# The first of two down projections in a two-layer trunk: from plain tiles to two by two blocks with seven products

## What the reference computes

```python
def _conv_ffn(x, w_up, conv_w, conv_b, w_down):
    hproj = _causal_dwconv(x @ w_up, conv_w) + conv_b
    gate, val = hproj[..., :D_FF], hproj[..., D_FF:]
    return (jax.nn.silu(gate) * val) @ w_down
...
        ffn = _conv_ffn(x, ffn_w_up[layer], ffn_conv_w[layer], ffn_conv_b[layer], ffn_w_down[layer])
        x = _layernorm(DN_ALPHA * x + ffn, ln2_g[layer], ln2_b[layer])
```

## Time and profile before

| | us |
|---|---|
| median of 3 runs (2879.61 to 2887.69) | 2882.05 |
| the profiled execution | 2882.41 |
| its span in the trace | 2880.6 |

### The profile page before, as it was taken

One profiled execution on the slowest core, in us unless ns is written; L12 is line 12 of the kernel. 1 busy time (PEld: TensorE's weight loads), 2 busy tenths in 40 slices (PEclk: granted clock), 3 DMA queues, 4 the chain that ended last, 5 costly groups with the idle time before them and its releaser, 6 DMA issues. The chain is left out here.

```text
span 2880.6 us, 45819 instructions
## 1 busy us (share of the span) xinstructions
PE 2789.7 (97%) x17767; PEld 2359.6 (82%) x17767; DVE 2050.4 (71%) x3198; ACT 1262.9 (44%) x2266; POOL 343.9 (12%) x273
## 2 busy tenths in 40 slices
PE   9999988999999999999999998999999999999998
PEld 7888877888888888888878886899987888887886
DVE  6544455675799999736489884355537999998978
ACT  5333245742444444322346753455443544444332
POOL 0000074230000000000000001455511000000001
PEclk9999999999999999999999999999999999999999
DMA  4333252524312222354422423522033122213852
GB/s 178 117 117 109 82 194 77 158 70 157 137 59 95 81 88 87 126 200 150 160 82 96 161 87 117 191 90 90 18 140 111 59 88 88 86 75 113 315 172 88
DMA packets 156454, 339.01 MB, mean 118 GB/s; under 512 B 35744, under 2 KB 69728, under 8 KB 145632
## 3 DMA queue, kind: packets, MB, share of 16 engines
q1 hardware_dynamic: 137680, 321.54, 31.6%
q10 hardware_dynamic: 18576, 14.75, 1.7%
HBM read 252.17 MB, written 84.05 MB: 117 GB/s over the span
## 5 line engine op out<-in xcount | busy, mean ns | idle before, releaser
L845 DVE TENSOR_TENSOR even_in_w_lo<-even_in_raw_left,even_in_w_hi 128x512 fp32r<-128x512 f32 x80 | 49.9, 686 | 88.2 <-ACT even_in_w_hi L770 88.2
L1625 PE MATMUL ffn_down_acc<-two_hi,ffn_a_hi 128*128 128x512 f32 x320 | 98.8, 390 | 2.3 <-DVEq L1692 1.5
L728 PE MATMUL even_in_acc<-even_in_w_hi,even_x_hi 128*128 128x512 f32 x256 | 99.6, 389 | 0.0
L729 PE MATMUL even_in_acc<-even_in_w_lo,even_x_hi 128*128 128x512 f32 x256 | 99.6, 389 | 0.0
L730 PE MATMUL even_in_acc<-even_in_w_hi,even_x_lo 128*128 128x512 f32 x256 | 99.6, 389 | 0.0
L1625 PE MATMUL ffn_down_acc<-two_lo,ffn_a_hi 128*128 128x512 f32 x320 | 98.5, 389 | 0.0
L1625 PE MATMUL ffn_down_acc<-two_hi,ffn_a_lo 128*128 128x512 f32 x320 | 98.5, 389 | 0.0
L1698 DVE TENSOR_TENSOR ffn_a_lo<-ffn_a_raw,ffn_a_hi 128x512 fp32r<-128x512 f32 x38 | 26.3, 692 | 101.4 <-ACT ffn_a_hi L1576 101.4
L3674 DVE SCALAR_TENSOR_TENSOR even_mixed<-even_mixed,odd_qkv_taps 128x1023 f32<-128x1023 f32 (+2 forms) x72 | 92.1, 1281 | 4.9 <-ACT even_mixed L3508 3.2
L1576 ACT CAST ffn_a_hi<-ffn_a_raw 128x512 fp32r<-128x512 f32 x38 | 23.7, 623 | 145.1 <-PE ffn_down_acc L1625 137.9
L1792 POOL TENSOR_TENSOR ffn_down_rstd<-ffn_down_rstd,ffn_down_power 128x1 f32<-128x1 f32 x7 | 7.5, 1066 | 662.6 <-DVE ffn_down_rstd L1727 662.6
(11 more groups left out here) (791 smaller groups left out, 9199.8 us busy)
## 6 DMA issues: line engine op xcount, KB each, us to landing
ffn_w_raw<-in_ffn_up SPq DMA_DIRECT2D x42, 1024.0 KB, 4.8
ffn_down_w_raw<-in_ffn_down SPq DMA_DIRECT2D x40, 512.0 KB, 3.4
hp<-even_in_stage SPq DMA_DIRECT2D x13, 1024.0 KB, 4.2
even_out_w_raw<-in_ev_w_out SPq DMA_DIRECT2D x22, 512.0 KB, 3.5
hidden<-even_mixed SPq DMA_DIRECT2D x22, 512.0 KB, 2.6
ffn_w_raw<-in_od_w_qkv SPq DMA_DIRECT2D x11, 1024.0 KB, 5.8
hidden<-odd_mixed SPq DMA_DIRECT2D x22, 512.0 KB, 2.6
ffn_a_raw<-hidden SPq DMA_DIRECT2D x42, 256.0 KB, 3.6
```

Source lines behind the costliest of these rows:

```text
L728: pe.matmul(to, hi[:, tok], wh, start=(opens and k == 0), stop=False, skip_group_check=not opens)
L729: pe.matmul(to, hi[:, tok], wl, start=False, stop=False, skip_group_check=not opens)
L845: dve.tensor_tensor(w_lo[:, p % 2, k], source(i)[:, k], f32(w_hi[:, p % 2, k]), ALU.subtract).then_inc(lo_ready, 1)
L1625: mm = pe.matmul(acc[:, t, n], aa[:, s, tok], ww[:, s, n * NB:(n + 1) * NB], start=(opening and aa is a_hi and ww is w_hi), stop=(last and ...
```

## The change

The first down projection now calls `project_blocks` too, with two new arguments. `space` gives it buffers in the bytes that later become the next stage's operand (`split_blocks`: the kept and raw blocks and one slot lie where the high and low parts of the next operand will be). `turning` makes it turn tiles 0 to 5 inside the last three chunks and copy them, load and split the next stage's first weights, leave tile 7 to `Late` (which now has only the right half of its columns to add, `half=True`), and return it. The opening loads of layer 0 become `OpeningWeights` and `OpeningRows`.

Inside `project_blocks`, for both layers: the two extra weight places are in the right half of `y[4..7]`, whose residual is loaded after them; gain and bias lie in the bytes of `w_kept` and are loaded after the sums that read it; chunk 39 has a buffer of its own (`ending`); the two PSUM halves change places.

```diff
@@ class Late
+        self.total, self.blocks = total, (1,) if half else (0, 1)
...
+        open_cols = y[:, t, self.blocks[0] * NB:D]
+        dve.scalar_tensor_tensor(out=open_cols, in0=open_cols, scalar=DN_ALPHA, in1=self.total,
                                  op0=ALU.mult, op1=ALU.add).then_inc(self.summed, 1)
         dve.wait_ge(self.summed, 1)
-        for b in range(2):
+        for b in self.blocks:
             dve.bn_stats(self.stats[:, t, b], y[:, t, b * NB:(b + 1) * NB]).then_inc(self.stats_done, 1)
@@ def project_blocks
-        hi_own, lo_own = (sc.sbuf(f"{part}_own", [P, 2 * D], F32R) for part in ("hi", "lo"))
+        with ExitStack() as shared:
+            w_kept = Scope(nc, shared, name).sbuf("w_kept", [P, KH, HALF])
+        affine = sc.sbuf("affine", [P, 2, D])
+        gain_b, bias_b = affine[:, 0], affine[:, 1]
+        ending = [sc.sbuf(f"ending{n}", [P, 2, HALF], F32R) for n in range(3)]
...
+        if space:
+            a_kept, a_raw, own = space
+        else:
+            (a_kept, own_a), (a_raw, own_w) = block_half(sc, "a_kept", "a"), block_half(sc, "a_raw", "w")
+            own = own_a + own_w
...
+        OWN = TT - 1 if turning else TT
+        EARLY = Late.FIRST if turning else 0
...
-            return (8, 9, 0, 1, 2, 3)[(q - PAIRS) % 6]
+            return (q - PAIRS) % 6
...
-            return (w_lent[:, e] if e < TT else w_own[:, e - TT])[:, 0:size(j)]
+            return (w_lent[:, e] if e < TT else y[:, 2 * e - 12:2 * e - 10, RIGHT])[:, 0:size(j)]
...
+            if s == 3:
+                return ending if c == CHUNKS - ENDING else own
...
+        def turn_place(t):
+            return acc[:, 0, t % 2 * 2:t % 2 * 2 + 2].rearrange("p b n -> p (b n)").rearrange("p (k t) -> p k t", t=P)
@@ sync
-            sp.wait_ge(w_lo_done, BLOCKS * (P7 + 1))
-            sp.dma_start(gain_b, gain.broadcast_to([P, D])).then_inc(affine_in, 16)
-            sp.dma_start(bias_b, bias.broadcast_to([P, D])).then_inc(affine_in, 16)
+            sp.wait_ge(w_sum, 4)
+            sp.wait_ge(w_lo_done, BLOCKS * P7 + 2)
             for t in range(HALF_T, TT):
                 sp.dma_start(y[:, t, RIGHT], resid[t * P:(t + 1) * P, RIGHT]).then_inc(right_in, 16)
...
+            sp.wait_ge(w_sum, 3 * BLOCKS + 2)
+            sp.dma_start(gain_b, gain.broadcast_to([P, D])).then_inc(affine_in, 16)
+            sp.dma_start(bias_b, bias.broadcast_to([P, D])).then_inc(affine_in, 16)
             for q in range(5 * BLOCKS, 6 * BLOCKS):
                 load_ring(q)
-            for t in range(TT):
+            if turning:
+                sp.wait_ge(used, CHUNKS - ENDING)
+                following.load(sp)
+            for t in range(OWN - 1 if turning else TT):
@@ scalar, behind the splits
+            if turning:
+                act.wait_ge(a_lo_done, CHUNKS)
+                act.wait_ge(w_lo_done, CHUNKS)
+            for t in range(EARLY):
+                act.wait_ge(turned, t + 1)
+                act.copy(hi[:, :, t * P:(t + 1) * P], turn_place(t))
+                act.copy(raw[:, :, t * P:(t + 1) * P], turn_place(t)).then_inc(raw_copied, 1)
+                if t == 1:
+                    following.split_hi(act)
@@ tensor
+            def turn(t):
+                pe.wait_ge(finished, t + 1)
+                if t < 2:
+                    pe.wait_ge(added, HALF_T * (P2 + 1))
+                else:
+                    pe.wait_ge(raw_copied, t - 1)
+                for k in range(KD):
+                    mm = pe.transpose(turn_place(t)[:, k], y[:, t, k * P:(k + 1) * P], ident[:])
+                mm.then_inc(turned, 1)
+
             for t in range(HALF_T):
                 for c in range(CHUNKS - ENDING, CHUNKS):
...
                         mm = step(c, k, t)
+                    if turning and t == HALF_T - 1 and c == CHUNKS - 2:
+                        turn(5)
                 mm.then_inc(tile_done, 1)
+                if turning and t < 2:
+                    turn(2 * t)
+                    turn(2 * t + 1)
+                if turning and t == 2:
+                    turn(4)
@@ vector
-            for t in range(HALF_T, TT):
+            for t in range(HALF_T, OWN):
                 add(P3, t - HALF_T)
...
                 finish(t)
+                if turning and t == HALF_T:
+                    following.split_lo(dve)
@@ build
-        down_first = first_rows(top, "ffn0_down", t["ffn_down0"], two)
-        rows = AheadRows(top, "ffn0_down", *split, hidden, down_first)
+        down_first = OpeningWeights(top, "ffn0_down", two, t["ffn_down0"].rearrange("(k p) n -> p k n", p=P))
+        rows = OpeningRows(top, "ffn0_down", *opened, hidden.rearrange("k p t -> p k t"))
...
-            late = project_out(nc, "ffn0_down", None, KF, k_rows(t["ffn_down0"]), x1, t["ln2_g"][0:1], t["ln2_b"][0:1],
...
+            late = project_blocks(nc, "ffn0_down", t["ffn_down0"].rearrange("(k p) n -> p k n", p=P), x1, t["ln2_g"][0:1],
+                                  t["ln2_b"][0:1], x2, one, down_first, rows, h_stored[0], rest, mixed[:, 0:KD], space,
+                                  (ident, x2_hi, mixed[:, 0:KD], qkv_first))
```

More of the change, by code:

```diff
@@ L1807, in project_out, with project_blocks @@
             return Late(y, gain_b, bias_b, stats, mean_var, rstd, power, ident, out, hi, raw, sums(TT - 1))
-def project_blocks(nc, name, w, resid, gain, bias, out, one, first, rows, a_stored, lead, lent):
+def project_blocks(nc, name, w, resid, gain, bias, out, one, first, rows, a_stored, lead, lent, space=None, turning=None):
     KH = KF // 2
@@ L1890, in slot @@
                 return rows.hi[:, cut], rows.lo[:, cut], first.hi[:, cut], first.lo[:, cut]
-            hi, lo = (part.rearrange("p (x k n) -> p x k n", x=2, n=HALF) for part in (one[:2] if s == 2 else (hi_own, lo_own)))
+            if s == 3:
+                return ending if c == CHUNKS - ENDING else own
+            hi, lo = (part.rearrange("p (x k n) -> p x k n", x=2, n=HALF) for part in one[:2])
             return hi[:, 0], lo[:, 0], hi[:, 1], lo[:, 1]
@@ L2192, in _, with block_half @@
             pool.wait_ge(power_set, 1)
-            for t in range(TT):
+            for t in range(OWN):
                 pool.wait_ge(rstd_ready, t + 1)
                 pool.tensor_tensor(rstd[:, t], rstd[:, t], power[:], ALU.pow).then_inc(rstd_done, 1)
+        if turning:
+            return Late(y, gain_b, bias_b, stats, mean_var, rstd, power, ident, out, hi, raw, bank(P3, HALF_T - 1), half=True)
+def block_half(sc, name, part, side=None):
+    held = sc.sbuf(name, [P, KF // 2, HALF], side=side)
+    return held, [sc.sbuf(f"own_{part}_{half}", [P, 2, HALF], F32R, side=side) for half in ("hi", "lo")]
 def project_heads(nc, name, a, w, resid, gain, bias, ident, out, hi, raw, place, first, following, held, a_held):
```

41 lines of the change are left out of this document (24 added, 17 removed).

## The result

The changed kernel takes 2856.73 us (median of 4 runs, 2854.19 to 2858.65) against 2882.61 us of the kernel before (median of 4); ratio 0.9908, 95% interval 0.9891 to 0.9925. In a second comparison, taken with the experiments, it was 2855.27 against 2884.33 us, 0.9901 (0.9884 to 0.9917). The forecast was 2856.4 us, range 2851 to 2865. The forecast time is right. Several of the terms behind it are not; they cancel in part, and the scatter between runs hides the rest.

What follows compares the result with a forecast made beforehand. TensorE was taken to bound both down projections. Terms -29.9, +4.9, +1.3 and small waits gave -25.3, with -0.4 behind the stage -25.7; from 2882.4, less 0.4 for the median, 2856.4 us, range 2851 to 2865.

Steps and rivals of the forecast that it cites:

- The body: First down projection's matmuls: 132 of 1056 removed at 0.2267 us each, the 48 transposes stay: -29.9 us.
- The joint: From up projection's fillers to first down projection's first matmul: +2.4 us length, +2.4 us half clock, together +4.9 us.
- Rival A: Joint into the first down projection stays short, only larger row splits lengthen it: +1.2 us, full clock, 2853; chance 0.13.
- +2.4 for the clock: Start of the first down projection: 12 matmuls at granted clock 0.50 after 3.90 us idle cost +2.4 us.
- small waits that vanish: Within the first down projection: TensorE not busy 1.84 us before, 0.19 in the second stage taken as model.
- The tail: End of the first down projection: VectorE ends last, TensorE idles 2.4 us instead of 1.0: +1.3 us.
- Rival B: Tail worse: half clock after the idle 2.4 us costs another 2.4 us, 2859, or tile 5 is late, similar; chance 0.15.
- Behind the stage: Next stage's second tile: VectorE has 1.2 us less work, of which only 0.4 can be had: -0.4 us.
- The last 230 us as long as now: End of the program, with the second down projection: no change in length expected.
- Edits at nothing: Both down projections: swapped PSUM halves, moved weight places, residual, gain, bias, chunk buffer and later next-stage weights cost nothing.
- Rival C: First third of the first down projection: VectorE, with late loads, stalls TensorE, 5 us of waiting, 2861; chance 0.09.
- Rival D: First third of the first down projection: loads get only 218 GB/s, 43 us more, 2900, slower; chance 0.03.

Runs made afterwards that it cites:

- the late load: Changed kernel with the first down projection's opening weights loaded one product (12 matmuls, 2.7 us) later: 2860.42 us, ratio 0.9917.
- the moved piece: Changed kernel with VectorE splitting the second opening row piece at the start of both down projections instead of before: 2855.33 us, ratio 0.9902.

## Why the forecast was right, and where it was not

- **The body, -29.9 us: right.** First to last instruction of the stage fell from 246.7 (1206.70 to 1453.43) to 217.3 us (1207.31 to 1424.62), 29.4, and by 30.1 in the second profiles. There is one wait of 1.06 us in it against waits of 0.82 and 0.73 before.
- **The joint, +4.9 us: the step that failed.** "So I take the second joint's measured length" took a disturbed joint as the model. The joint measured +0.4 us and full clock in place of +2.4 and +2.4. The mechanism (late weights, long joint, half clock) is real, as the late load shows; but the new form does not bring it. Rival A's place was right, and its reason too: VectorE's queue sets the joint once the weights are in time, as the moved piece shows. It had given 2.7 us idle; it was 1.84, since both forecast and rival left out that ScalarE no longer waits for both weight pieces, which gave VectorE 1.1 us back.
- **What the disturbed joint was.** In the three profiles with the old first stage and no added waits it is 5.37, 5.59 and 4.44 us; in nine of the ten with the new one it is 2.2 to 3.5, in the tenth, with added waits, 4.22; and in one profile of the kernel before with 76 idle waits it was 3.43. Work and loads are the same with and without these waits, so the place of the code is the likely cause; one profile each does not prove it. In the three long cases the instruction packet lies 0.1 to 0.2 us ahead of the issue of the two loads, in no other profile does it lie there. That it makes the joint long is not shown, and the 4.22 us without it speak against it as the only way.
- **Half clock was priced too high.** At the start of these stages the loads set the pace, so TensorE's lost 2.4 us come back: all of it in the second stage (201 matmuls in 48.2 us at either clock, and 1.76 us of waiting at 2662.59 once the clock was full), all but 0.3 to 0.5 us in the late-weights run. The sum also booked both sides: +2.4 for the clock and 1.6 us for small waits that vanish, though the second stage was free of them at least in part because of that clock.
- **The tail, +1.3 us: right in layout, +1.1 measured.** VectorE ends last; TensorE is idle 2.12 us at the next stage's start instead of 1.02, and tile 5's margin is 1.6 us where 1.2 was laid out. Rival B's first half came true in most profiles: 1.6 us of half clock behind 2.1 us idle, not 2.4. It had been given 0.15 on one row against it.
- **Behind the stage, -0.4: right** (1.30 to 0.92 us).
- **"The last 230 us as long as now": wrong.** 1.4 us shorter: the joint 2.2 us less, the rest 0.8 more. The forecast took the second joint for a fixed property of its stage, and it was not.
- **Edits at nothing: right to the resolution of the times** (ratio 0.9997, 3 us either way); the rows show 0.5 to 1.0 us behind the second joint. **Rival C** came in small: 1.06 us, not 5, and of its two reasons the late loads are shown. **Rival D** did not come: the stage's first third moved 328 GB/s.

From the fillers to the next stage -25.3 us was forecast and -28.0 came in the first profiles: the joint 4.5 us less, the tail 0.2 less, the body 2.1 more (-29.4 where -29.9 and 1.6 us of vanishing small waits had been booked). Behind the stage it was +0.5 over two profiles of each kernel where -0.4 was forecast, by the half clock in one of them; at the end -1.4 where nothing was. The rows make that -29.2 us over two profiles against -25.7 forecast; the medians -25.9 in one comparison and -29.1 in the other. So the forecast is 3.5 us off by the rows, and that it meets the first median within 0.4 us is luck.

## What to carry to other kernels

A stage that already runs in the new form is a good model for its body, but its edges belong to the program around it: look at what an odd length there consists of (here the issue of two loads in 1.50 us instead of 0.90, and the second of them 2 us late) before it is carried over. Before a slow clock is priced, look at what sets the pace behind it: where TensorE soon waits for loads, the time lost at half clock is waiting saved. Once matmuls are removed, add up the next engine's busy time: here, with VectorE at 190 us, the gain of further matmuls ended after 21 us, and the loads of the first third are nearer still. Work moved to GpSimd beside a VectorE that reads two inputs can cost more than it saves.

## What the hardware showed

- Half clock behind an idle time of about 2 us is not settled by its length. Of the idle times at the three joints over 14 profiles, none of 14 up to 1.77 us was followed by it, 9 of 20 between 1.79 and 2.13 us were, and of 8 longer ones all but those of 2.75 and 2.97 us. The 9 are 4 of 14 up to 2.04 us and 5 of 6 at 2.12 or 2.13, all of these at the exit of the stage, so length and place are not told apart; one kernel gave both at the same place.
- What half clock costs hangs on the work behind it: 1.6 us in the next stage (278.3 against 276.7 us), nothing in the second down projection (201 matmuls in 48.2 us at either clock).
- VectorE's two-input split stood still for 2.2 of the 2.42 us of GpSimd's.
- The same two loads of 512 KB reached ScalarE 4.0 and 5.3 us after the issue in the changed kernel, 4.8 and 7.3 in the kernel before, with the same queue and bytes; 76 waits on TensorE's queue, 880 us before them, made it 4.0 and 5.4 again.
